# Hybrid mLSTM, short-convolution and cross-attention layer: first rows and unit reordered, gates in column tiles, last tile's turn moved, last norm in halves

## The reference, cut to what matters

```python
def memory_kv(mem, g_mem, w_mem_kv):            # 256 memory tokens
    kv = rms_norm(mem, g_mem) @ w_mem_kv
    mk, mv = jnp.split(kv, 2, axis=-1)
...
def hybrid_layer(x, mem_k, mem_v, C0, n0, m0, conv0, g_norm, w_in, b_if, g_head, conv_w, conv_b, w_out):
    xn = rms_norm(x, g_norm)
    proj = xn @ w_in
    (q, k, v, o_pre, z_ml, i_pre, f_pre, b_g, c_g, xc, z_cv, q_x, z_x) = split_in(proj)
    i_pre = i_pre + b_if[:ML_HEADS]
    logf = jax.nn.log_sigmoid(f_pre + b_if[ML_HEADS:])
    h, C, n, m = mlstm_chunkwise(heads(q), heads(k) * (ML_HEAD_DIM ** -0.5), heads(v), i_pre, logf, C0, n0, m0)
    h = rms_norm(jax.nn.sigmoid(heads(o_pre)) * h, g_head.reshape(ML_HEADS, ML_HEAD_DIM))
    y_ml = h.reshape(B, T, ML_WIDTH) * jax.nn.silu(z_ml)
...
    y = jnp.concatenate([y_ml, y_cv, y_xa], axis=-1) @ w_out
    return (x + y, C, n, m, conv_new)
...
y_prompt = rms_norm(hp, g_final); y_sample = rms_norm(hs, g_final)
```

## Time and profile before

| | us |
|---|---|
| median of 3 runs (2146.47 to 2149.42) | 2149.39 |
| the profiled execution | 2147.59 |
| its span in the trace | 2145.8 |
| PE busy | 2093.5 (98%) |
| DVE, ACT, POOL busy | 1363.7, 959.3, 896.2 |

### The profile page before, as it was taken

The page is one execution under the profiler, slowest core; times in us unless marked ns, Lnnn a source line. Parts: engine busy times, 40 slices in busy tenths (PEclk is TensorE's granted clock), DMA queues, the critical chain, the costliest instruction groups (busy, mean ns, idle before and its releaser), DMA issues. The chain is left out here.

```text
span 2145.8 us, 34710 instructions
## 1 busy us (share of the span) xinstructions
PE 2093.5 (98%) x12689; PEld 1954.2 (91%) x12689; DVE 1363.7 (64%) x2140; ACT 959.3 (45%) x1982; POOL 896.2 (42%) x741
## 2 busy tenths in 40 slices
PE   7899999999999999999999999999999899999997
PEld 4899999999999999999999999978878788888885
DVE  6577676697777766877787766443344455555554
ACT  5454445545444455454454454433332344334331
POOL 1455555584555555755555555211000422222210
PEclk9999999999999999999999999999999999999999
DMA  6334334434333344343334444555454766666654
GB/s 212 121 123 123 122 120 132 135 111 134 123 123 117 121 143 135 120 137 118 123 113 123 136 137 133 187 173 174 129 175 143 204 174 199 199 191 194 196 148 91
DMA packets 344007, 311.99 MB, mean 145 GB/s; under 512 B 43120, under 2 KB 306192, under 8 KB 343840
## 3 DMA queue, kind: packets, MB, share of 16 engines
q1 hardware_dynamic: 337728, 289.79, 45.1%
q0 software_dynamic: 2912, 9.64, 1.4%
q10 hardware_dynamic: 3200, 10.36, 1.2%
HBM read 224.82 MB, written 84.92 MB: 144 GB/s over the span
## 5 line engine op out<-in xcount | busy, mean ns | idle before, releaser
L672 PE MATMUL bank<-xh,wh 128*128 128x352 f32 x2688 | 870.0, 324 | 10.0 <-ACT snap L844 8.3
L674 PE MATMUL bank<-xh,wl 128*128 128x352 f32 x2688 | 865.8, 322 | 0.0
L673 PE MATMUL bank<-xl,wh 128*128 128x352 f32 x2688 | 863.5, 321 | 0.0
L1025 DVE TENSOR_TENSOR wl<-raw,wh 128x512 fp32r<-128x512 f32 x384 | 417.4, 1089 | 208.1 <-ACT wh L809 206.8
L672 PEld LDWEIGHTS bank<-xh,wh 128*128 128x128 f32 x2688 | 504.9, 188 | 12.2 <-ACT snap L844 9.5
L674 PEld LDWEIGHTS bank<-xh,wl 128*128 128x128 f32 x2688 | 507.3, 189 | 0.0
L673 PEld LDWEIGHTS bank<-xl,wh 128*128 128x128 f32 x2688 | 506.2, 188 | 0.2 <-issue 0.2
L844 ACT ACTIVATE snap<-bank 128x352 f32<-128x352 f32 x384 | 178.5, 465 | 373.4 <-PE bank L674 373.3
L809 ACT ACTIVATE wh<-raw 128x512 fp32r<-128x512 f32 x384 | 241.2, 630 | 169.5 <-PE bank L674 154.5
L1025 DVE TENSOR_TENSOR wl<-wt,wh 128x512 fp32r<-128x512 f32 x288 | 237.2, 828 | 112.9 <-ACT wh L809 112.2
L620 POOL TENSOR_TENSOR stage<-snap 128x352 f32<-128x352 f32 x96 | 97.8, 1018 | 460.3 <-ACT snap L844 457.2
(11 more groups left out here) (311 smaller groups left out, 2725.3 us busy)
## 6 DMA issues: line engine op xcount, KB each, us to landing
raw<-in_w_in SPq DMA_DIRECT2D x72, 1024.0 KB, 5.6
raw<-in_w_in SPq DMA_DIRECT2D x48, 512.0 KB, 5.6
scr_vo<-stage SPq DMA_DIRECT2D x48, 352.0 KB, 6.9
scr_qk<-stage SPq DMA_DIRECT2D x48, 352.0 KB, 6.1
raw<-scr_qk SPq DMA_DIRECT2D x16, 1024.0 KB, 6.9
area<-scr_vo SPq DMA_DIRECT2D x16, 1024.0 KB, 9.5
scr_z<-stage SPq DMA_DIRECT2D x24, 352.0 KB, 2.2
scr_xa<-stage SPq DMA_DIRECT2D x24, 352.0 KB, 2.4
```

Source lines behind the costliest of these rows:

```text
L672: pe.matmul(out, wh[:, b, k, :], xh[:, b, k, :], start=(first and k == 0), stop=False, skip_group_check=True)
L673: pe.matmul(out, wh[:, b, k, :], xl[:, b, k, :], start=False, stop=False, skip_group_check=True)
L674: m = pe.matmul(out, wl[:, b, k, :], xh[:, b, k, :], start=False, stop=(k == 3), skip_group_check=True)
L1025: dve.tensor_tensor(low, source(q, b), high.bitcast(F32), ALU.subtract).then_inc(S["w_low"], 1)
```

## The change

First rows: 7 slots instead of 4 (`SLOTS`), and SP's order of loads is rows 0, gain, 1, 2, then key/value weights 0, gain, rows 3, 4, weights 1, rows 5, 6, weights 2, row 7, and the first unit's weights. ACT loads the table of the square root ahead of the first row. PE makes 30 transposes of the identity into bank 7 (`WARM`). DVE copies block 1 out before it norms block 2. Gates: a unit without blocks; their 8 columns stay f32 in `gall`, and 16 f32 matmuls, for k in 4 for j in 4 column tiles of 32, write bank 6; only the first 8 of a tile's 32 rows are gates, the rest are neighbours or zeros. One evacuation of 128 partitions replaces two of 16, four DMAs replace one.

```diff
+SLOTS = 7
+WARM = 30
...
-            for b, parts in ((0, ((6, A11), (7, S1))), (1, ((6, A12),)), (2, ((7, A22),))):
-                pe.wait_ge(S["w_low"], CN.block[q] + b + 1)
-                for where, x in parts:
-                    for k in range(4):
-                        pe.matmul(bank[where][:, 0:HALF], wh[:, b, k, :], xh[:, x, k, :], start=(b == 0 and k == 0), stop=False)
...
+            for k in range(4):
+                for j, (at, x) in enumerate(((0, A11), (4, A12), (0, S1), (KD, A22))):
+                    m = pe.matmul(bank[6][32 * j:32 * j + 32, 0:HALF], gate_weights[:, 8 * (at + k):8 * (at + k) + 32],
+                                  xf[:, x, k, :], start=(k == 0), stop=(k == 3), skip_group_check=True)
+            m.then_inc(S["gates_summed"], 1)
...
+        for k in range(WARM):
+            pe.transpose(bank[7][:, 0:P], ident[:, :], ident[:, :])
...
+                    act.activation(gst, bank[6][:, 0:HALF], ACT.Identity, bias=bif[:, 0:1]).then_inc(S["gate_evacuated"], 1)
+                    act.wait_ge(S["gate_evacuated"], s + 1)
+                    for j in range(4):
+                        at = PASS * s + HALF * (j // 2)
+                        act.dma_start(w["gate"][8 * (j % 2):8 * (j % 2) + 8, at:at + HALF],
+                                      gst[32 * j:32 * j + 8, :]).then_inc(S["gate_out"], 16)
...
         act.wait_ge(S["eps_ready"], 1)
+        act.activation(sd1[:, 0:1], eps[:, :], ACT.Sqrt).then_inc(S["sqrt_table"], 1)
...
-        for b in range(3, 7):
+        for b in (3, 4):
             first_high(b)
             w_high(0, b)
-        act.wait_ge(S["wkv_used"], KD)
-        for i in range(4):
-            act.activation(kvs[:, i, :], bank[4 + i][:, :], ACT.Copy).then_inc(S["kv_copied"], 1)
 
         def memory_out(q, i):
+            if q == 0 and i == 2:
+                for b in (5, 6):
+                    first_high(b)
+                    w_high(0, b)
+            if q == 0 and i == 3:
+                act.wait_ge(S["wkv_used"], KD)
+                for n in range(4):
+                    act.activation(kvs[:, n, :], bank[4 + n][:, :], ACT.Copy).then_inc(S["kv_copied"], 1)
...
-                w_high(q + 1, i)
+                w_high(q + 1, i - 3 if q == 0 else i)
...
         for u in range(NR):
+            if u == 2:
+                rows_back(1)
             norm_rows(u)
-            if u:
+            if u not in (0, 2):
                 rows_back(u - 1)
```

```diff
-    OUTS = [*range(NT - 1), NT, NT - 1]
...
+                if t == NT - 1:
+                    out_part(t - 1, 8)
+                    out_part(t - 1, 9)
+                    turn_y(t)
+                    out_part(t - 1, 10)
+                    out_part(t - 1, 11)
+                    pe.wait_ge(S["y_gated"], 2 * t + 2)
                 unit_update(t, u)
-                for g in range(8, 16):
+                for g in range(12 if t == NT - 1 else 8, 16):
                     out_part(t - 1, g)
...
+        for g in range(16):
+            out_part(NT - 1, g)
+            if g == 7:
+                turn_n()
+        for g in range(16):
+            out_part(NT, g)
...
+            if t == NT - 1:
+                update(t, 8)
+                add(t - 1, (0,))
+                y_gate(t)
+                y_low(t)
+                unit_update(u)
+                unit_second_half(u)
+                add(t - 1, (1,))
+                unit_y_gate(u)
+                break
...
+        for n in range(2):
+            c = slice(512 * n, 512 * (n + 1))
+            dve.scalar_tensor_tensor(acc[0:TS, NT % ACC, c], acc[0:TS, NT % ACC, c], ors[0:TS, NT:TILES], gf[0:TS, c], ALU.mult,
+                                     ALU.mult).then_inc(S["out_ready"], 1)
```

More of the change, by code:

```diff
@@ L250, in __init__ @@
         for s, kind, i in JOBS:
-            n = 3 if kind == "gate" else 7
+            n = 0 if kind == "gate" else 7
             self.convs.append(convs)
@@ L335, in project @@
     srow = gt[0:88, :]
-    gst = work[0:16, 0:PASS]
+    gst = work[:, 0:HALF]
     N = len(JOBS)
@@ L378, in blocks @@
     def blocks(q):
-        return 0 if q >= N else 3 if JOBS[q][1] == "gate" else 7
+        return 0 if q >= N or JOBS[q][1] == "gate" else 7
     def first_of_pass(q):
@@ L441, in _ @@
         sp.wait_ge(S["bif_zero"], 1)
-        sp.dma_start(bif[0:8, :], b_if[0].rearrange("(a b) -> a b", b=1)).then_inc(S["bif_loaded"], 16)
+        for half in range(2):
+            sp.dma_start(bif[64 * half:64 * half + 8, :], b_if[0].rearrange("(a b) -> a b", b=1)).then_inc(S["bif_loaded"], 16)
         def load(q):
@@ L799, in w_high @@
         def w_high(q, b):
-            if b >= blocks(q):
+            if not 0 <= b < blocks(q):
                 return
-            if JOBS[q][1] == "gate":
-                act.wait_ge(S["gd_ready"], 1)
-            elif b in (0, 3, 5):
+            if b in (0, 3, 5):
                 act.wait_ge(S[f"raw_loaded{CN.pair[q] % 2}"], CN.loaded[q])
@@ L822, in evacuate @@
                 if i == 2:
-                    act.wait_ge(S["product"], CN.block[q] + 3)
+                    act.wait_ge(S["gates_summed"], s + 1)
                     wait(act, S["post"], CN.posted[q][0])
@@ L1018, in _ @@
         dve.memset(bif[:, :], 0.0).then_inc(S["bif_zero"], 1)
+        dve.memset(gall[:, 12:15], 0.0).then_inc(S["gall_zero"], 1)
         def w_low(q, b):
-            if b >= blocks(q):
+            if not 0 <= b < blocks(q):
                 return
@@ L2020, in _ @@
                 out_norm(t - 2)
-        for t in range(NT - 2, TILES):
+        for t in range(NT - 2, NT):
             out_norm(t)
+        pool.wait_ge(S["last_squared"], 1)
+        pool.tensor_scalar(oms[:, NT:TILES], oss[:, NT:TILES], 1.0 / D, EPS, ALU.mult, ALU.add).then_inc(S["last_begun"], 1)
+        pool.wait_ge(S["last_mean"], 1)
+        pool.tensor_tensor(ors[:, NT:TILES], osl[:, 1:2], half[:, 0:1], ALU.pow).then_inc(S["out_rstd"], 1)
     @block.tensor
@@ L2376, in score_weights, with add @@
                                      ALU.mult, ALU.mult).then_inc(S["sw_ready"], 1)
-        def add(s):
-            r = slice(0, width(OUTS[s]))
+        def add(s, halves=(0, 1)):
+            r = slice(0, width(s))
             dve.wait_ge(S[f"acc_loaded{s % ACC}"], 16 * (s // ACC + 1))
-            for n in range(2):
+            for n in halves:
                 c = slice(512 * n, 512 * (n + 1))
```

136 lines of the change are left out of this document (71 added, 65 removed).

## The result

| | us |
|---|---|
| median after, 7 runs (2127.91 to 2138.75) | 2131.69 |
| median before, 7 runs beside them (2146.47 to 2151.75) | 2149.42 |
| ratio, 95% interval | 0.9923 [0.9905, 0.9940] |
| profiled execution after, its span | 2129.8, 2128.0 |

A forecast was written before the change was run, and what follows sets the result against it. PE was taken as supplied except at both ends, plus half-clock work. First rows and unit 0 13.3, gates 4.25, end 4.8: 22.4 us off, giving 2125.2 from the profile, 2127.0 from the median; forecast 2126.0, range 2119 to 2136.

The forecast's parts named there:

- the front does not move: First rows: loads, not the chain, set the first key/value matmul; 6.4 us stay, 2131.6 us; chance 0.04.
- Part 1: First rows: first key/value matmul at 12.6 instead of 16.48, 3.9 us; with a warm clock unit 0 begins 6.4 earlier.
- The 2.5 us for a warm clock: First key/value stretch: if warm-up transposes have raised the clock by 12.6, its 7.04 us shrink by some 4.5, gaining 2.5.
- I take them as counting: First rows: transposes count as busy work that raises PE's clock; otherwise the sum is 2.5 us smaller.
- Part 2: Unit 0 to key transposes: snaps moved ahead of later splits and copies, 15.2 us instead of 22.1, gaining 6.9.
- Part 3: Projection gates: 32 records in 2.4 us instead of 5.13; gains 0.65 us in pass 0, 1.8 twice, 4.25 in all.
- lands 2.6 later: Pass 0: the keys' store, awaited by the gates' evacuation, lands 2.6 us after issue, leaving 0.65 us gain.
- the clock falls in the longer waits: PE's waits before product 2 drop the clock, 1.7 us lost each; one to three falls, 2126.9 to 2130.3; chance 0.14.
- Part 4: The end: moved turn brings the last matmul 4.3 us nearer, shorter work behind PE gives 0.5; 4.8 in all.
- Everywhere else it is supplied: Between the two ends: PE has no notable waits, so the middle is worth what PE executes there.
- the column tiles did run side by side: Gates: the rival had tiles one after another, 0.293 us a record, 9.4 us, 2145.2, no change; chance 0.04.
- their loads of 0.11 us were hidden: Gates: the rival had column-tile weight loads exposed, 32 x 0.11 us more, 5.9 us, 2134.7; chance 0.04.

The follow-up runs named there:

- front_alone: The kernel before with only the first-rows edits (slots, load order, first copies, warm-ups) and the new order of unit 0: 2139.56 us, ratio 0.9952.
- no_warm: The changed kernel without the 30 warm-up transposes: 2135.70 us, ratio 0.9940 to the kernel before.
- gates_one_tile: gates_apart with 16 more gate matmuls, all in the first column tile, overwritten by the real ones: 2155.06 us, ratio 1.0029 to the kernel before.
- gates_apart: The changed kernel with gates evacuated into the tanh tile, so ACT no longer waits there for the key/value stores: 2122.55 us, ratio 0.9880 to the kernel before.
- Tail_alone: The kernel before with only the tail edits (tile 15's turn amid tile 14's groups, sample rows last, last norm in halves): 2144.73 us, ratio 0.9978.
- filled: The changed kernel with 34 warm-up transposes and 14 and 6 more behind blocks 0 and 1: 2133.08 us, ratio 0.9928 to the kernel before.

## Why the prediction was right, and where it was not

The direction was right and the time is in the range, but the forecast is nearer to it than its working was: two terms lost 8 us against the sum, and 3.3 came back from things that it did not hold. The median of 2131.69 is also just what the rival "the front does not move" had, 2131.6, and there the number misleads: the front moved, by 3.6 us at the first key/value matmul.

**Part 1.** The chain to the first key/value matmul was right: 12.86 against 12.6. The 2.5 us for a warm clock were right where it stayed up (unit 0 at 45.0 in front_alone) and wrong in most traces. The step that failed is the one behind "I take them as counting": they count, but PE then idled 0.8, 2.0 and 0.8 us before the first key/value matmul, and I had looked only at whether the clock rises, not at whether it is still up when needed. It cost 2.0 us; no_warm shows in its trace that the warm-ups are still worth 1.7 us at unit 0 (48.74 against 47.04).

**Part 2.** Right: 15.1 us from unit 0 to the key transposes against 15.2. On the way, the snap of product 2 begins at 6.4 us for 6.1 and product 6 at 13.1 for 13.3, behind a wait of 0.5 for DVE's output of product 3, as foreseen.

**Part 3.** The gates' price was right (2.57 against 2.4, and gates_one_tile shows what it rests on), and so were passes 1 and 2: PE's wait was 1.19 and 1.18 us instead of 2.0 (a slip: by its own terms, 0.76 and the 0.93 from 4.74 to 5.67, it would have been 1.7), the gain in pass 1 9.87 less 7.78, 2.1 for 1.8. The term that failed is pass 0, "lands 2.6 later": it took 6.5, because the change itself moves the store into a stretch in which the DMA engines are full; from its landing to product 2 are 5.4 us, as foreseen. I had 0.65 us of gain there; the trace shows 2.9 us of loss to product 2 and 2.3 more for what follows at half clock, which is the rival "the clock falls in the longer waits" for this wait. Together 5.9 us on that term, and gates_apart, which takes away only this wait, returns 9.1 us by the medians. In the traces it is 6.6 without the front's 1.6; from span to span it is 7.8, because gates_apart then lost 3.1 us by the pace of the units and won 2.7 behind the projection.

**Part 4.** Right: 5.2 us in the trace for 4.8 (4.5 to PE's last matmul for 4.3, 0.7 behind it for 0.5). Tail_alone gave 3.9 by the medians and the same 5.2 in its trace.

**What I had not counted** is between the passes and the tail: 1.5 us of pace in favour of after (the last eight units 13.35 us each, 13.53 before), and a clock that falls in other places of the attention and the first tiles of `recur` in each trace. Of the 3.3 us that came back, 2.8 are there and 0.4 in the tail. "Everywhere else it is supplied" was wrong: behind the projection PE waited 3.0, 4.2, 2.4, 3.3, 2.1 and 2.6 us before the change, with the clock at half for 20.5 us in all up to tile 15. Of the rivals, the column tiles did run side by side and their loads of 0.11 us were hidden, the loads of the first rows did not hold the front, and the clock fell in the long wait of pass 0 but not in those of 1.2 us. The late landing of the store stood in none of them.

## What to carry to other kernels

When a step is moved forward, look up what runs on the DMA engines at its new place, not how long its transfer took at the old one, and then who waits for it through a semaphore that counts more than they need. Give a tile with an early user a place of its own, and keep DMA issues out of an engine's list ahead of what another engine waits for. A wait of PE can cost more than its length, because what follows it can run at half clock: the one of 5.9 us cost 2.3 more. But judge a filler by the time at the end of the stage and not by the clock in a window: here a later wait took the gain.

## What the runs showed of the hardware

- Transposes of the identity alone raised the granted clock to 2.4 GHz (the eight at 7.87 take 1.09 us, 1.94 without them), and with the same first instructions one trace keeps it at 12 us (gates_apart) and another loses it (after).
- With every operand there and the clock granted in full, a unit of 84 matmuls of 352 columns takes 13.35, 13.44 or 13.53 us for whole stretches; filled lost 2.9 us to after by it over 16 units.
- f32 matmuls in four column tiles of 32 start in fours, within 0.02 us, every 0.30 us at 352 columns; the same ones in a single tile start one by one every 0.30 us, while the record of each is 459 ns long in both.
- A 512 KB store landed in 2.6 us beside little other traffic (DMA share 0.34) and in 6.3 to 6.5 us in a full stretch (0.98).
